# One chain of sums for two norms of x, even chunks summed first, and seven slots in the feed-forward rooms

## What is computed

```python
def rms_norm(x, g):
    y = x * lax.rsqrt(jnp.mean(x * x, axis=-1, keepdims=True) + EPS)
    return y * g

# end of the first model, start of the second
x = rms_norm(h, norm_final)
px = (rmsnorm(x, norm1_g[l]) * (1.0 + sc1) + sh1) @ w_in[l] + b_in[l]
...
x = x + g1 * (y_x @ w_out[l])
x = x + g2 * swiglu(rmsnorm(x, norm2_g[l]) * (1.0 + sc2) + sh2, w_gu[l], w_down[l])
```

## Time and profile before

| | |
|---|---|
| median of three runs | 2669.48 us |
| the profiled execution, its own time | 2661.06 us |
| its span, first to last instruction | 2659.3 us |
| mean granted clock of TensorE | 0.912 |
| PE busy | 2299.1 us, 86% |
| DVE busy | 1154.5 us, 43% |
| ACT busy | 884.4 us, 33% |
| read from HBM | 672.15 MB, 253 GB/s |

### The profile page before, as it was taken

The page is one execution under the profiler, slowest core; times in us unless marked ns, Lnnn a source line. Parts: engine busy times, 40 slices in busy tenths (PEclk is TensorE's granted clock), DMA queues, the critical chain, the costliest instruction groups (busy, mean ns, idle before and its releaser), DMA issues. The chain is left out here.

```text
span 2659.3 us, 45347 instructions
## 1 busy us (share of the span) xinstructions
PE 2299.1 (86%) x19616; PEld 1828.5 (69%) x19616; DVE 1154.5 (43%) x2041; ACT 884.4 (33%) x1471; POOL 58.3 (2%) x78
## 2 busy tenths in 40 slices
PE   6999688888796799887999999886896998996998
PEld 6957465665462787675767676553766998866998
DVE  4344635323320552545323232333756554755554
ACT  4423232133210443332222221322534443534442
POOL 0000000000000000000000000000000000000000
PEclk9988898898998899988999999887888999988999
DMA  6575698899999556847999999976503644404650
GB/s 225 159 242 204 222 384 336 332 369 391 402 388 398 192 188 227 292 156 280 394 394 386 393 393 379 394 276 235 197 17 109 224 167 145 139 5 141 208 167 24
DMA packets 254368, 676.25 MB, mean 254 GB/s; under 512 B 12624, under 2 KB 65872, under 8 KB 254160
## 3 DMA queue, kind: packets, MB, share of 16 engines
q1 hardware_dynamic: 238832, 614.74, 62.5%
q0 software_dynamic: 15328, 58.50, 6.5%
HBM read 672.15 MB, written 1.05 MB: 253 GB/s over the span
## 5 line engine op out<-in xcount | busy, mean ns | idle before, releaser
L434 PE MATMUL bank<-xx,high 128*128 128x256 f32 (+1 forms) x3296 | 634.3, 294 | 59.5 <-DVE xx L570 37.1
L434 PEld LDWEIGHTS bank<-xx,high 128*128 128x128 f32 (+1 forms) x3296 | 524.6, 195 | 117.3 <-issue 76.7
L434 PE MATMUL bank<-xx,low 128*128 128x256 f32 (+1 forms) x1648 | 475.8, 289 | 0.0
L434 PEld LDWEIGHTS bank<-xx,low 128*128 128x128 f32 (+1 forms) x1648 | 321.8, 195 | 1.6
L385 DVE TENSOR_TENSOR low<-lane,high 128x1024 fp32r<-128x1024 f32 (+1 forms) x112 | 130.7, 1170 | 374.6 <-ACT high L376 374.6
L376 ACT ACTIVATE high<-lane 128x1024 fp32r<-128x1024 f32 (+1 forms) x112 | 112.9, 1012 | 334.0 <-PE bank L434 334.0
L434 PE MATMUL bank<-hx,high 128*128 128x256 f32 x1056 | 200.6, 291 | 6.3 <-DVE low L385 6.3
L434 PEld LDWEIGHTS bank<-hx,high 128*128 128x128 f32 x1056 | 166.5, 193 | 24.2 <-issue 15.2
L434 PE MATMUL bank<-hx,low 128*128 128x256 f32 x528 | 150.4, 285 | 0.0
L1229 ACT ACTIVATE hs<-bank 64x256 f32<-64x256 f32 x64 | 24.2, 377 | 312.3 <-PE bank L1216 312.2
L1236 DVE TENSOR_TENSOR hs<-hs,bank 64x256 f32<-64x256 f32 x64 | 27.1, 423 | 222.7 <-ACT hs L1229 222.5
(11 more groups left out here) (510 smaller groups left out, 4211.4 us busy)
## 6 DMA issues: line engine op xcount, KB each, us to landing
ring__11<-in_expert_w_gu SPq DMA_DIRECT2D x52, 1024.0 KB, 11.1
ring__10<-in_expert_w_gu SPq DMA_DIRECT2D x51, 1024.0 KB, 11.4
ring__12<-in_expert_w_gu SPq DMA_DIRECT2D x51, 1024.0 KB, 11.0
ring__50<-in_expert_w_gu SPq DMA_DIRECT2D x26, 1024.0 KB, 10.7
ring__10<-in_expert_w_down SPq DMA_DIRECT2D x26, 1024.0 KB, 9.1
ring__150<-in_expert_w_gu SPq DMA_DIRECT2D x26, 1024.0 KB, 12.0
ring__49<-in_expert_w_gu SPq DMA_DIRECT2D x25, 1024.0 KB, 10.8
ring__12<-in_expert_w_down SPq DMA_DIRECT2D x25, 1024.0 KB, 9.7
```

Of the source, the lines that this page charges most:

```text
L434: done = pe.matmul(out, a.bitcast(F32R), b.bitcast(F32R), start=it["start"] and k == 0 and q == 0 and not halves, stop=stop)
```

## The change

- `Norm.order` sums the even chunks first where nothing was summed early.
- `TwoNorms` replaces norm_x and the tail's first norm. It squares x once as it is and once times the gain g (for DVE times g squared), both before x is scaled, and PE sums both, into two banks. From the first mean plus epsilon it gets the reciprocal; times the second mean this is the second norm's mean; its root and reciprocal times the first norm's root give the factor that the split applies to x as it stands. The gain of the split is the product of both gains (`gg`).
- `settle` scales x itself, one chunk of 128 by 256 behind each item of the projection.
- ret opens with `x_done(0)` and squares each chunk as it is done; so does the tail's first mixer. The room norm_x is gone, so the mixer's room follows moe's directly.
- The feed-forward rooms have seven slots, not eight.

```diff
@@ Norm
+            def order(self):
+                return range(self.early, KC) if self.early else [*range(0, KC, 2), *range(1, KC, 2)]
...
-                for c in range(self.early, KC):
+                for c in self.order():
@@
+        class TwoNorms(Norm):
+            def __init__(self, name, xs, n, sq, sq2, rs1, rs2, g, g2, ready):
+                super().__init__(name, xs, n, sq, rs2, ready)
+                self.sq2, self.rs1, self.g, self.g2 = sq2, rs1, g, g2
+
+            def squares(self, e, which):
+                if which:
+                    e.tensor_tensor(self.g2, self.g, self.g, MUL).then_inc(*v_step.up((self.name, "g2")))
+                    e.wait_ge(*v_step.at((self.name, "g2")))
+                for c in range(which, KC, 2):
+                    events_wait(e, self.ready(c))
+                    z = self.x[:, c, :]
+                    if which:
+                        e.tensor_tensor(self.sq[:, c, :], z, z, MUL)
+                        i = e.scalar_tensor_tensor(self.sq2[:, c, :], z, self.g2[:, c:c + 1], z, MUL, MUL)
+                    else:
+                        e.activation(self.sq[:, c, :], z, ACT.Square)
+                        i = e.activation(self.sq2[:, c, :], z, ACT.Square, scale=self.g[:, c:c + 1])
+                    i.then_inc(*(sq_v if which else sq_a).up((self.name, c)))
+
+            def sums(self, pe):
+                keys = [(self.name, i) for i in range(2)]
...
+                for c in self.order():
+                    pe.wait_ge(*(sq_v if c % 2 else sq_a).at((self.name, c)))
+                    for key, z in zip(keys, (self.sq, self.sq2)):
+                        i = pe.matmul(self.bk[key][:, 0:self.n], ones, z[:, c, :], start=c == 0, stop=c == KC - 1)
+                i.then_inc(*csum.up(self.name))
+
+            def root(self, act):
+                act.wait_ge(*rstd.at((self.name, "mean")))
+                act.activation(self.rs, self.rs, ACT.Sqrt, bias=eps).then_inc(*root.up(self.name))
+                act.activation(self.rs1, self.rs1, ACT.Sqrt).then_inc(*root.up((self.name, "first")))
+
+            def rstd(self, dve):
+                sums = [self.bk[self.name, i][:, 0:self.n] for i in range(2)]
+                dve.wait_ge(*csum.at(self.name))
+                dve.tensor_scalar(self.rs1, sums[0], 1.0 / DM, EPS, MUL, ADD).then_inc(*rstd.up((self.name, "first")))
...
+                dve.reciprocal(self.rs1, self.rs1).then_inc(*rstd.up((self.name, "squared")))
...
+                dve.scalar_tensor_tensor(self.rs, sums[1], 1.0 / DM, self.rs1, MUL, MUL).then_inc(*rstd.up((self.name, "mean")))
...
+                dve.wait_ge(*root.at(self.name))
+                dve.reciprocal(self.rs, self.rs).then_inc(*rstd.up((self.name, "second")))
+                dve.wait_ge(*rstd.at((self.name, "second")))
+                dve.wait_ge(*root.at((self.name, "first")))
+                dve.tensor_tensor(self.rs, self.rs, self.rs1, MUL).then_inc(*rstd.up(self.name))
+                dve.wait_ge(*rstd.at(self.name))
+
+            def settle(self, dve):
+                for c in range(KC):
+                    z = self.x[:, c, :]
+                    dve.scalar_tensor_tensor(z, z, self.g[:, c:c + 1], self.rs1, MUL, MUL).then_inc(*nrm.up((self.name, "x", c)))
+                    yield
@@ ret
-            norm = Norm("ret", x, T, tmp, rs, lambda c: [])
+            norm = Norm("ret", x, T, tmp, rs, x_ready)
@@ mixer
+            if v and not L:
+                norm = TwoNorms(name, xs, T, yt, tm, rs, rM, V("norm_final"), g2, x_ready)
+                norm.split_to(tm, xh, xl, [(0, T, lambda c: gg[:, c:c + 1], gains(L, 0, 0, v)[0][3])])
@@ mixer, dve
                 dve.wait_ge(*gm_v.at(L))
+                settle = iter(())
+                if v and not L:
+                    gm = mods[:, 96:128].rearrange("p (i c v) -> p i c v", i=2, c=8)
+                    dve.tensor_tensor(gg, gm[:, 0, :, v], norm.g, MUL).then_inc(*nrm.up((name, "gain")))
+                    settle = norm.settle(dve)
                 norm.rstd(dve)
@@ mixer, dve, in the loop over items
                     at = it["at"]
+                    next(settle, None)
                     if at > ends["gate"] + 2:
@@ x_ffn
-            room = Room(f"ffn{L}", 8, before, opened)
+            room = Room(f"ffn{L}", 7, before, opened)
@@ stages
-        room, early, x_done, s = ret(room, x_done(7))
+        room, early, x_done, s = ret(room, x_done(0), x_done)
...
-        room, opened, s = norm_x(room, x_done(7))
-        stages.append(s)
-        early = None
+        early, opened = None, x_done(0)
```

More of the change, by code:

```diff
@@ L585, in done @@
                 return [(xl_, (self.name, (c + 1) * self.np - 1))]
+        class TwoNorms(Norm):
[18 more added lines that the diff above has]
+                keys = [(self.name, i) for i in range(2)]
+                for key in keys:
+                    self.bk.next(key)
+                    for s, k in self.bk.freed(key):
+                        pe.wait_ge(*s.at(k))
+                for c in self.order():
[11 more added lines that the diff above has]
+                dve.tensor_scalar(self.rs1, sums[0], 1.0 / DM, EPS, MUL, ADD).then_inc(*rstd.up((self.name, "first")))
+                self.bk.free((self.name, 0), (rstd, (self.name, "first")))
+                dve.wait_ge(*rstd.at((self.name, "first")))
+                dve.reciprocal(self.rs1, self.rs1).then_inc(*rstd.up((self.name, "squared")))
+                dve.wait_ge(*rstd.at((self.name, "squared")))
+                dve.scalar_tensor_tensor(self.rs, sums[1], 1.0 / DM, self.rs1, MUL, MUL).then_inc(*rstd.up((self.name, "mean")))
+                self.bk.free((self.name, 1), (rstd, (self.name, "mean")))
+                dve.wait_ge(*root.at(self.name))
[9 more added lines that the diff above has]
+                    yield
@@ L1637, in build, with ret @@
         tab_in = sig("ret_tab_in")
-        def ret(before, opened):
+        def ret(before, opened, x_ready):
             room = Room("ret", 4, before, opened)
@@ L1913, in mixer @@
             nw = get("nw", 2, 2, P)
+            gg, g2 = (get("gain", KC) for _ in range(2)) if v and not L else (None, None)
             if states_only:
@@ L1942, in mixer @@
             bcv, bu, bq, bk_ = V("bc", 4 * L, 4), V("bu", 2 * L, 2), V("bq", 4 * L, 4), V("bk", 4 * L, 4)
-            norm = Norm(early_in or name, xs, T, yt, rs, x_ready or (lambda c: []), early=4 if early_in else 0, bk=bk)
-            norm.split_to(tm, xh, xl, gains(L, 0, 0, v))
+            if v and not L:
+                norm = TwoNorms(name, xs, T, yt, tm, rs, rM, V("norm_final"), g2, x_ready)
+                norm.split_to(tm, xh, xl, [(0, T, lambda c: gg[:, c:c + 1], gains(L, 0, 0, v)[0][3])])
+            else:
+                norm = Norm(early_in or name, xs, T, yt, rs, x_ready or (lambda c: []), early=4 if early_in else 0, bk=bk)
+                norm.split_to(tm, xh, xl, gains(L, 0, 0, v))
             def biased(d, f, b):
@@ L2805, in x_ffn @@
             return room, early, x_done, in_one_go(s)
[L2810 to L2828, removed]
         def final(before, opened, early_name, x_ready):
@@ L2889, in build @@
         stages.append(s)
-        room, opened, s = norm_x(room, x_done(7))
-        stages.append(s)
-        early = None
+        early, opened = None, x_done(0)
         for L in range(2):
-            room, early, x_done, s = x_mixer(L, room, ended(x_done, early) if early else opened, early, x_done if early else None)
+            room, early, x_done, s = x_mixer(L, room, ended(x_done, early) if early else opened, early, x_done)
             stages.append(s)
```

2 lines of the change are left out of this document (added).

## The result

The changed kernel took 2657.36 us in the median of 20 runs (2634.86 to 2663.68), the kernel before 2670.9 us in as many (2657.97 to 2684.37). The ratio is 0.9933, interval 0.9913 to 0.9952: 13 to 23 us less. A second comparison gave 0.9944 (0.9913 to 0.9974). The forecast was 0.9923.

What follows compares the result with a forecast made beforehand. PE, busy 86% of the span, was taken to stand at short handovers waiting on chains and weight loads. 9.5 - 1.4 + 1.8 + 9.6 + 1.0 = 20.5 us off the 2669.48 median gave 2649.0, range 2636 to 2660.

Steps and rivals of the forecast that it cites:

- A: Tail's entry: new chain longer than costed, first part falling to about 4 us, total to 16: 2653.5; chance 0.15.
- B: Feed-forward entries: loads still wait, slot not common or held by other loads, gain only 9.9: 2659.6; chance 0.06.
- Tail's entry: Final mixture to tail's first split: one chain replaces two norms, split at 1853.35 not 1862.90; 9.5 us gained, bounds 7.0 to 11.
- Settling: Tail's first projection: eight scalings of x behind its first eight items cost 1.4 us, bounds 0 and 1.6.
- Retention's entry: Start of retention: squaring from the first add lets sums start at 875.4, not 877.26; 1.8 us gained, bounds 0.8 and 2.
- Seven slots: Both feed-forward entries: first load takes a common slot, ACT's weight wait goes, 4.8 us each; 9.6 gained, bounds 9 and 10.
- Clock: Both feed-forward entries: PE returns before the granted clock falls, so early matmuls run faster; 1.0 us gained, bounds 0 and 1.8.
- C: Feed-forward up and down products: seven slots starve the stages, costing 58 us, 2707, slower by 1.4%; chance 0.04.
- Its sign: Feed-forward stretch of 193 us: PE busy for clearly less than 189 us would show the prediction wrong.
- D: Transfer lands in half the time, clock stays up at both stages: 25 us or more, 2644 and below; chance 0.10.
- The rule on consistent bubbles: Feed-forward stages: bubbles on the engine to be saturated mean too few buffers; eight slots show none, seven should show none.

## Why the prediction was right, step by step

The forecast held: 2649.0 (2636 to 2660) against 2657.36, ratio 0.9923 against 0.9933 and 0.9944. By the profiles the gain is 15.5 us where 20.5 stood, so it was a third too high, and one step has the sign wrong. That the time lies in the range has some luck in it: it is 2.6 us under the upper bound, and nearer to the figures of rivals A (2653.5) and B (2659.6) than to the forecast. What tells these apart is the trace and not the time.

1. *Tail's entry, 9.5 us:* 9.85, and by the chain that was written: 18.12 us and not 18.4, the transfer landing in 9.15 against the 9.25 taken. What the Trainium skill states for such a transfer, 6.15 us (DMA: Bandwidth & Descriptors, section Bandwidth), was not met here with others in flight. The sums ended 1.4 us ahead of it, as costed: they ran at a granted clock of 0.50 for 4.8 us and the rest of them at 1.00, 9.5 us in all. The 9.8 us written for 5.5 slow ones comes to 10.0 with its own figures (0.80 and 0.50 us each).
2. *Settling, -1.4:* -0.9, by the run without it. It sits where it was put, at the last tap.
3. *Retention's entry, 1.8:* 2.3, just above the upper bound of 2. The first sum starts 1.35 us behind the first addition and not 3.08, so 1.7 us came as costed. The sums of the kernel after took 5.48 us where the earlier trace rows has 6.11, since the clock rose sooner: from 2 to 4 us behind their start it was granted at 0.60, and before at 0.50. That part varies from profile to profile: the entry took 7.0 to 8.5 us in the eight that open at the first addition, and 8.7 to 10.2 in the five that don't, 2.0 us between the means.
4. *Seven slots, 9.6:* 9.9 at the two entries, 4.98 and 4.89. The mechanism (slot 7 not common, SP in line behind it) is right.
5. *Clock, +1.0, bounds 0 and 1.8:* this step failed, in two places. At the entries it had the sign wrong. PE did come back earlier, but the clock was then at 0.50 under it for longer: until 6.3 us behind PE's return at the first entry, where it was 5.8, and for 6.8 us at the second, where it was 5.6. At the first it fell before PE came back, at the second only just behind it. Up to the step to the down product the stages took 0.3 and 0.8 us more. And the bounds looked only at the entry, and left out that the rest of the stage has a wait that can tip the clock: behind it the stages took 2.5 and 1.3 us more. Together that is 2.8 and 2.0. The second mixer took 1.0 us more as well. There the granted clock lacked 23.9 us of 1.00, summed over its length, against 22.2 before, and 18.0 against 17.4 while PE was busy, so 0.6 of the 1.0 is seen as clock and the rest stays open. In all -5.8.

By the profiles, 9.85 - 0.8 + 2.3 + 9.9 - 5.8 = 15.5 us, in place of 20.5. The step on the clock is off by 6.8 us, and the other four together gave 1.7 more than costed.

The rivals: A (16 us, a longer chain; 20.5 with 9.5 cut to 4 is 15.0) has the size but not the cause, as the chain took what was costed. B (the loads still wait) is out by SP's queue and the wait gone at ACT. C (starving) is out by the stages of 203 to 205 us with seven slots. Its sign, PE busy for clearly less than 189 us of 193, seems to be there in 187.91, but that window takes in 1.0 us of the entry's idle time and a wait of 0.92 that the earlier trace rows leaves out; placed alike the two kernels have the same. D, more than costed, was not seen. The rule on consistent bubbles cited there (the Trainium skill, Perfetto Trace Analysis, section Optimization Strategy) agrees in so far as no bubbles came.

## What to carry to other kernels

Follow a handover's chain past the compute to the queue that issues its loads: a buffer that isn't free early holds every load behind it, and one slot fewer can be the faster ring. Then look for short waits inside the dense stretch behind the handover, each a place where the clock may fall once what precedes it has moved; taking out one of 3.17 us gave 3.1 and 3.4 us where the clock had not fallen at it, and 4.7 to 6.1 where it had. Until that wait was gone, the time could not tell the slots' gain (0.9997 alone). Compare profiles stretch by stretch and not by their spans, and place the windows alike, by an event of the stage.

## What the runs showed of the hardware

- Of TensorE's clock: behind an idle time of 3.17 us within a stream that is otherwise full, the granted clock stayed at 1.00 in 4 stages of 16 and fell to 0.50 in the 12 others, for 3.4 to 6.8 us. What follows to the end of the stage then took 1.3 to 2.7 us longer. With the wait gone it fell in none of ten.
- One stretch of fox ran at a granted clock of 0.66, the mean of pieces at 1.00 and at 0.50, with PE busy all the time, in the profile of the kernel after, and at 1.00 in that of before. Fox as a whole took 240.6 to 258.7 us for the same instructions. By size this can make most of the spread of single executions, 2651 to 2688 us of the kernel before; that it does is not shown.
- A transfer of 1 MB beside others landed in 9.15 and 9.25 us; two records of the fp32 sums (128x256) took 0.85 us with the granted clock low and 0.43 with it high.
